# Wide up products of the later expert passes: two token blocks by two chunks with seven products

## The reference, cut to what matters

```python
def swiglu(h, w_gate, w_up, w_down):
    return (jax.nn.silu(h @ w_gate) * (h @ w_up)) @ w_down

def moe_swiglu(h, router_w, router_b, w_gate, w_up, w_down):   # D_FF_EXPERT = 1408, N_EXPERTS = 8, TOP_K = 2
    t = h.reshape(B * S, Dm)
    logits = (t @ router_w).astype(jnp.float32) + router_b.astype(jnp.float32)
    ...                                                        # combine: softmax of the two best logits
    for e in range(N_EXPERTS):
        out = out + combine[:, e:e + 1] * swiglu(t, w_gate[e], w_up[e], w_down[e])
```

## Time and profile before

| | |
|---|---|
| device time, median of three runs | 1250.8 us (1249.82 to 1252.56) |
| profiled execution: its own time | 1252.16 us |
| profiled execution: span, granted clock | 1250.6 us, 0.997 |
| busy share of TensorE, VectorE, ScalarE, GpSimd | 98%, 54%, 22%, 7% |
| bytes moved by DMA over the span | 368.62 MB, mean 295 GB/s |
| chain that ended last, by engine | TensorE 90%, VectorE 4%, DMA 3% |

### The profile page before, as it was taken

The page is one execution under the profiler, slowest core; times in us unless marked ns, Lnnn a source line. Parts: engine busy times, 40 slices in busy tenths (PEclk is TensorE's granted clock), DMA queues, the critical chain, the costliest instruction groups (busy, mean ns, idle before and its releaser), DMA issues.

```text
span 1250.6 us, 26663 instructions
## 1 busy us (share of the span) xinstructions
PE 1224.5 (98%) x10620; PEld 929.6 (74%) x10620; DVE 671.3 (54%) x1676; ACT 278.5 (22%) x739; POOL 88.4 (7%) x157
## 2 busy tenths in 40 slices
PE   6999999999999999999999999999999999999997
PEld 4758888999999867799999998777654455445444
DVE  5365563888888756556766786874541011101104
ACT  4332203311211424540000004375300000000001
POOL 0010100000000010000000000100011100110120
PEclk9999999999999999999999999999999999999999
DMA  9999884477777683146777685796599999999994
GB/s 344 413 400 415 326 304 150 167 274 274 274 257 278 242 293 126 36 166 222 276 276 281 256 320 197 292 374 177 197 384 395 416 399 398 399 422 399 399 398 175
DMA packets 74853, 368.62 MB, mean 295 GB/s; under 512 B 8739, under 2 KB 8995, under 8 KB 50082
## 3 DMA queue, kind: packets, MB, share of 16 engines
q1 hardware_dynamic: 56594, 271.22, 57.7%
q0 software_dynamic: 18192, 96.47, 20.1%
HBM read 347.60 MB, written 20.06 MB: 294 GB/s over the span
## 4 chain that ended last, share of the span: by engine, by line
PE 90%; DVE 4%; DMA 3%; ACT 1%; SPq 1%; issue 0%; DVEq 0%; POOLq 0%; ACTq 0%
PE banks L970 21%; PE banks L1298 13%; PE banks L698 13%; PE banks L957 12%; PE banks L1347 9%; PE banks L1322 5%; PE banks L723 4%; PE banks L829 2%; PE banks L787 2%; DMA side<-ada 2%; PE banks L1037 2%; PE banks L888 1%; DVE side L1744 1%; DMA ring<-stream 1%; PE banks L868 1%; PE banks L904 1%
## 5 line engine op out<-in xcount | busy, mean ns | idle before, releaser
L1744 DVE CUSTOM_DVE_ANT_0 side<-side 128x1024 f32<-128x1024 f32 x128 | 151.0, 1219 | 30.0 <-DMA side<-ada 29.9
L1298 PE MATMUL banks<-ring,arena 128*32 128x512 f32 x1536 | 166.3, 592 | 0.0
L957 PE MATMUL banks<-arena,ring 128*128 128x256 f32 x704 | 158.6, 379 | 0.0
L957 PEld LDWEIGHTS banks<-arena,ring 128*128 128x128 f32 x704 | 130.7, 190 | 16.1
L698 PE MATMUL banks<-h,ring 128*128 128x256 f32 x640 | 142.3, 381 | 0.3
L698 PEld LDWEIGHTS banks<-h,ring 128*128 128x128 f32 x640 | 119.7, 190 | 18.9 <-issue 1.8
L1298 PEld LDWEIGHTS banks<-ring,arena 128*32 128x32 f32 x1536 | 49.7, 110 | 111.5 <-issue 110.4
L2368 DVE TENSOR_TENSOR arena<-arena,banks 128x256 f32<-128x256 f32 (+1 forms) x48 | 15.2, 330 | 177.7 <-ACT arena L1681 177.7
L698 PE MATMUL banks<-arena,ring 128*128 128x256 f32 x384 | 84.3, 380 | 0.7 <-ACT arena L1480 0.5
L970 PEld LDWEIGHTS banks<-h,ring 128*128 128x128 f32 x672 | 81.4, 192 | 2.2
L970 PE MATMUL banks<-arena 128*128 128x128 f32 x672 | 81.9, 275 | 0.0
(11 more groups left out here) (334 smaller groups left out, 1547.5 us busy)
## 6 DMA issues: line engine op xcount, KB each, us to landing
ring<-stream SPq DMA_DIRECT2D x247, 512.0 KB, 5.6
ring<-experts SPq DMA_DIRECT2D x96, 1024.0 KB, 21.2
side<-ada POOLq DMA_DIRECT2D x64, 1024.0 KB, 7.4
side<-experts SPq DMA_DIRECT2D x24, 1024.0 KB, 22.9
arena<-experts SPq DMA_DIRECT2D x8, 1024.0 KB, 24.5
yrows<-side POOLq DMA_DIRECT2D x1, 6144.0 KB, 42.7
hrows<-side POOLq DMA_DIRECT2D x1, 5632.0 KB, 23.3
arena<-lasts SPq DMA_DIRECT2D x8, 512.0 KB, 24.4
```

The costliest lines, as they stand in the source:

```text
L957: last = pe.matmul(banks[:, 4 + c // 2, (c % 2) * T:(c % 2 + 1) * T], ring[:, s, c * P:(c + 1) * P], hid[:, j % 2, :], start=first and c % ...
L1298: ins = pe.matmul(banks[BLOCK * j:BLOCK * (j + 1), t, :], hg[:, t, k, :], ring[:, m, (j % 2) * 512:(j % 2 + 1) * 512], start=(k == 0), sto ...
L1744: dve.tensor_tensor_reduce(weights, weights, cond[:, 0 if layer0 else 1, :], 1.0, 0.0, ALU.mult, ALU.add, accum_out=msum[:, n:n + 1]).then ...
```

## The change

In passes 1 to 7 the wide up products of token blocks 0 and 1 are made in a form with fewer block products. Two chunks of input features (a pair, c = 0 to 3) and two token blocks form a 2x2 block matrix, and the gate and up weights of the two chunks another. Eight products of 256 columns become seven, three of them with weights as they are and four with sums of weights (`wsum`, one buffer for each of the four sums, in the memory of `h` and of `early`). VectorE makes four sums of the token blocks for the whole pass (`tksum`) and four sums of weights for each pair. It makes pair 0's sums ahead of `weighted_rows` and the others behind it. The products add up in six half banks, and nine operations of VectorE combine them (`combine_seven`). The third token block keeps its 512-column matmuls, in bank 5: first in pairs 0 to 2, last in pair 3. The narrow products move to banks 4 and 3. Wide slots are given back four at a time, near the end of a pair. GpSimd's load of the next token rows, and so what follows on its queue, waits for `s_prod`, which the first third-block matmul of pair 3 raises for the ninth time in a pass. Pass 0 keeps its old form.

```diff
+        wsum = [h[:, 0:4, :], h[:, 4:8, :], region(20, [QUADS, WIDE]), region(16, [QUADS, WIDE])]
+        tksum = var[:, :].rearrange("p (i c b) -> p i c b", i=4, b=BLOCK)
...
+        def wide_blocks(k):
+            chunk = ring[:, 2 * k:2 * k + 2, :].rearrange("p s (b n) -> p (s b) n", b=2)
+            return chunk[:, :, 0:WIDE], chunk[:, :, WIDE:2 * WIDE]
...
                 pool.wait_ge(rows_stored, 64 * (p + 1))
+                pool.wait_ge(s_prod, 9 * (p + 1))
                 pool.wait_ge(s_hg_low, p + 1)
                 rows_load(hrows[bass.ds((p + 1) * CAP, CAP), :])
...
+            def up_wide_seven(p):
+                pe.wait_ge(s_hg_low, p + 1)
+                pe.wait_ge(s_pickT_act, 1)
+                pe.wait_ge(s_tksum, 4 * p)
+                for c in range(KC // 2):
+                    (gate1, up1), (gate2, up2) = wide_blocks(2 * c), wide_blocks(2 * c + 1)
+                    start, stop = c == 0, c == KC // 2 - 1
...
+                    pe.wait_ge(slot_full[4 * c], 16 * (before[4 * c] + p + 1))
+                    if not stop:
+                        third_block(0)
+                    pe.wait_ge(slot_full[4 * c + 2], 16 * (before[4 * c + 2] + p + 1))
+                    if not stop:
+                        third_block(1)
+                    product(0, 0, hg[:, 0, 2 * c, :], gate1)
+                    product(1, 0, hg[:, 0, 2 * c + 1, :], gate2)
+                    product(2, 0, tksum[:, 3, c, :], up2)
+                    pe.wait_ge(s_wsum, 16 * p - 16 + 4 * c + 1)
+                    product(1, WIDE, tksum[:, 0, c, :], wsum[0], False)[-1].then_inc(s_prod, 1)
+                    pe.wait_ge(s_wsum, 16 * p - 16 + 4 * c + 2)
+                    product(0, WIDE, tksum[:, 1, c, :], wsum[1], False)[-1].then_inc(s_prod, 1)
+                    pe.wait_ge(s_wsum, 16 * p - 16 + 4 * c + 3)
+                    made = product(2, WIDE, tksum[:, 2, c, :], wsum[2], False)
...
+                    pe.wait_ge(s_wsum, 16 * p - 16 + 4 * c + 4)
+                    made = product(3, 0, hg[:, 1, 2 * c + 1, :], wsum[3])
+                    if stop:
+                        made[1].then_inc(s_up, 2)
+                        made[3].then_inc(s_up, 2)
+                        made = third_block(0)
+                        made[0].then_inc(s_prod, 1)
...
+                        for ins in third_block(1):
+                            ins.then_inc(s_up, 1)
...
+                def token_block_sums():
+                    dve.wait_ge(s_hg_low, p + 1)
...
+                    dve.tensor_tensor(tksum[:, 0], a21, a22, ALU.add).then_inc(s_tksum, 1)
+                    dve.tensor_tensor(tksum[:, 2], a11, a21, ALU.subtract).then_inc(s_tksum, 1)
+                    dve.wait_ge(s_tksum, 4 * p - 3)
+                    dve.tensor_tensor(tksum[:, 1], tksum[:, 0], a11, ALU.subtract).then_inc(s_tksum, 1)
+                    dve.wait_ge(s_tksum, 4 * p - 1)
+                    dve.tensor_tensor(tksum[:, 3], a12, tksum[:, 1], ALU.subtract).then_inc(s_tksum, 1)
...
+                def block_sums(c):
+                    n = 16 * p - 16 + 4 * c
+                    (gate1, up1), (gate2, up2) = wide_blocks(2 * c), wide_blocks(2 * c + 1)
+                    dve.wait_ge(slot_full[4 * c], 16 * (before[4 * c] + p + 1))
+                    if c:
+                        dve.wait_ge(s_prod, 9 * p + 2 * c - 1)
+                    dve.tensor_tensor(wsum[0], up1, gate1, ALU.subtract).then_inc(s_wsum, 1)
+                    dve.wait_ge(slot_full[4 * c + 2], 16 * (before[4 * c + 2] + p + 1))
+                    if c:
+                        dve.wait_ge(s_prod, 9 * p + 2 * c)
+                    dve.wait_ge(s_wsum, n + 1)
+                    dve.tensor_tensor(wsum[1], up2, wsum[0], ALU.subtract).then_inc(s_wsum, 1)
+                    if c:
+                        dve.wait_ge(slot_used[4 * c - 3], before[4 * c - 3] + 2 * p + 2)
+                    dve.tensor_tensor(wsum[2], up2, up1, ALU.subtract).then_inc(s_wsum, 1)
+                    if c:
+                        dve.wait_ge(slot_used[4 * c - 1], before[4 * c - 1] + 2 * p + 2)
+                    dve.wait_ge(s_wsum, n + 2)
+                    dve.tensor_tensor(wsum[3], gate2, wsum[1], ALU.subtract).then_inc(s_wsum, 1)
...
                 if first:
+                    hidden(0, 0, WIDE)
+                    hidden(1, WIDE, NARROW)
+                else:
+                    token_block_sums()
+                    block_sums(0)
                     weighted_rows(p)
-                hidden(0, 0, WIDE)
-                hidden(1, WIDE, NARROW)
+                    for c in range(1, KC // 2):
+                        block_sums(c)
+                    combine_seven()
+                    hidden_wide_seven()
+                    hidden_narrow_seven()
                 rows_turned(p)
...
             expert_pass(0, True)
+            dve.wait_ge(rows_stored, 64)
             passes = dve.value_load(ints[0:1, NTAB:NTAB + 1], min_val=EXPERTS, max_val=EXPERTS + EXTRA)
```

More of the change, by code:

```diff
@@ L1283, in combine, with up_wide @@
                                 ins.then_inc(s_lastscatter, 1)
-            def up_wide(p, first):
+            def up_wide(p):
                 pe.wait_ge(s_hg_low, p + 1)
-                if not first:
-                    pe.wait_ge(s_pickT_act, 1)
                 for k in range(KC):
-                    if first and k == 4:
+                    if k == 4:
                         pe.wait_ge(s_hg_high, 1)
@@ L1313, in up_narrow @@
                 for t in range(BLOCKS):
+                    if t == BLOCKS - 1 and not first:
+                        pe.wait_ge(s_comb, 9 * p - 8)
                     for k in range(KC):
@@ L1333, in pick_transposes, with expert_down @@
                 last.then_inc(s_picktr, 1)
-            def expert_down(p, first, last):
+            def expert_down(p, first, last, first_pass):
                 for c in range(first, last):
@@ L1351, in expert_down @@
                                 ins.then_inc(s_down, 1)
[L1352 removed]
+                            elif t == BLOCKS - 1 and m in slot_used:
                                 ins.then_inc(slot_used[m], 1)
             def expert_pass(p, first=False):
[L1356 removed]
+                if first:
+                    up_wide(p)
+                else:
+                    up_wide_seven(p)
                 up_narrow(p, first)
@@ L2381, in expert_pass @@
                     dve.wait_ge(consts_set, 6)
-                if not first:
-                    weighted_rows(p)
-                hidden(0, 0, WIDE)
-                hidden(1, WIDE, NARROW)
+                def token_block_sums():
+                    dve.wait_ge(s_hg_low, p + 1)
+                    pairs = [hg[:, t].rearrange("p (c e) b -> p c e b", e=2) for t in range(2)]
+                    a11, a12, a21, a22 = (pairs[t][:, :, e, :] for t in range(2) for e in range(2))
+                    dve.tensor_tensor(tksum[:, 0], a21, a22, ALU.add).then_inc(s_tksum, 1)
[4 more added lines that the diff above has]
+                    dve.tensor_tensor(tksum[:, 3], a12, tksum[:, 1], ALU.subtract).then_inc(s_tksum, 1)
@@ new lines, in turned, with hidden_wide_seven @@
+                def turned(t, at, w, n):
+                    dve.wait_ge(s_hid, n)
+                    dve.transpose(mhidT[:, t, at:at + w], mhid[:, t, at:at + w]).then_inc(s_hidT, 1)
+                def hidden_wide_seven():
+                    n = HIDS * p
+                    dve.wait_ge(s_msilu, n + 1)
+                    dve.tensor_tensor(mhid[:, 2, 0:WIDE], msg[:, 2, :], banks[:, 5, WIDE:2 * WIDE], ALU.mult).then_inc(s_hid, 1)
+                    for t in range(2):
+                        dve.wait_ge(s_msilu, n + t + 2)
+                        dve.wait_ge(s_comb, 9 * p)
+                        dve.tensor_tensor(mhid[:, t, 0:WIDE], msg[:, t, :], mhid[:, t, 0:WIDE], ALU.mult).then_inc(s_hid, 1)
+                        turned((2, 0)[t], 0, WIDE, n + t + 1)
+                    turned(1, 0, WIDE, n + 3)
@@ new lines, in hidden_narrow_seven @@
+                def hidden_narrow_seven():
+                    n = HIDS * p + BLOCKS
+                    for t, w in ((0, 2), (2, 1)):
+                        dve.wait_ge(s_msilu, n + t + w)
+                        dve.tensor_tensor(mhid[:, t:t + w, WIDE:QF], msg[:, t:t + w, 0:NARROW], narrow_blocks(t, w)[:, :, NARROW:2 * NARROW],
+                                          ALU.mult).then_inc(s_hid, w)
+                    for t in range(BLOCKS):
+                        turned(t, WIDE, NARROW, n + max(t, 1) + 1)
```

88 lines of the change are left out of this document (75 added, 13 removed).

## The result

The changed kernel takes 1256.29 us, the median of five runs (1255.05 to 1258.92). Its ratio to the kernel before is 1.0043, 95% interval 1.0027 to 1.0059: slower by some 5.4 us. The forecast was 1251.9 us; the time lies within the range given, but not within the forecast's own. That it lies within the range is luck: the upper end stood for slower sums of VectorE, which did not come, and the loss is another. The profiled execution took 1255.05 us, with a span of 1253.4 us and a granted clock of 0.999. It entered pass 0 2.4 us earlier than the one before, by scatter ahead of the change, so its passes lost more than the two spans show.

A forecast was written before the change was run, and what follows sets the result against it. TensorE, busy 98%, was taken to bound the kernel. Pass 1's +3.35 us less 6 x 0.37 for steady passes gave +1.1; 1253.3 for the profiled execution, 1251.9 us forecast as median, range 1248.2 to 1257.5.

The forecast's parts named there:

- the range given: Whole kernel: 1248.2 to 1257.5 us, from a time without sum stalls, with some scatter, to the sums' upper price.
- the forecast's own: Whole kernel: the favoured case's own range, 1249.5 to 1253.5 us, at a chance of 0.55.
- the upper end: VectorE's sums at their upper price, 1.28 us long and 1.20 apart; the range reaches 1257.5 us.
- Steady pass: Later passes: pair 3's last sum about 1 us late, wide part 20.2 instead of 20.60 us, gaining 0.37 a pass.
- Rival C: VectorE's sums follow each other without overlap; a pass loses 0.5 us, pass 1 4.6, time 1258.4 us; chance 0.17.
- Rival D: TensorE's clock falls in the stall of every pass, costing 1.7 us each, time about 1264 us; chance 0.08.
- Pass 1: First changed pass: late token sums and weight sums end the wide part at 964.5 instead of 961.16, losing 3.35 us.
- What costs nothing: Combining, down-part sums, moved row loads and gathers, slot returns: all hidden or in time, the gathers landing at about 1233.
- signs of being wrong: Wide part 19 us with end near 1237, sums 1.25 apart throughout, clock under 1.00 within passes, or TensorE waiting on DMA.
- The queue: Weight transfers need about 44.7 us a pass against TensorE's 42.64, falling behind 2.1 a pass; a large saving meets their end.
- rival B: Sums do not hold TensorE up, but gathered rows land about 1232.4 and mixing ends at 1237.5: 1249.0 us; chance 0.20.

The follow-up runs named there:

- one sum less: Changed kernel with VectorE's third weight sum left out in pairs 1 to 3 (output partly wrong): 1249.47 us in one run.
- gathers later: Changed kernel with GpSimd waiting for the narrow part's end after loading the rows, so the gathers fall beside the down products: 1256.42 us in one run.
- the gathers first: Changed kernel, third block first in pair 3, gathers written to ring slots and issued ahead of pass 8's unused row load: 1247.30 us, ratio 0.9977 to the kernel before.
- pass 1 written out: Changed kernel with TensorE's pass 1 written out ahead of its loop, which then starts at pass 2: 1256.61 us in one run.
- the moved wait alone: Kernel before with only POOL's new wait for the wide part's end before it loads the next rows: 1254.11 us, ratio 1.0021.
- plain loads: Changed kernel with the four indirect gathers replaced by four plain POOL loads of the same size (wrong output rows): 1253.72 us in one run.
- both edits: Changed kernel with the third block first in pair 3 and pass 1's weight and token sums made earlier: 1251.01 us, ratio 0.9995 to the kernel before.
- gathers to other memory: Changed kernel, third block first in pair 3, pass 1's sums earlier, gathers written to ring slots emptied by pair 0: 1248.03 us, ratio 0.9971 to the kernel before.
- half the weights: Changed kernel, third block first, pass 1's sums earlier, gathers to ring slots, pass 7 loading half its weight bytes (wrong output): 1241.81 us in one run.
- all together: Changed kernel, third block first, early pass 1 sums, gathers to ring slots before the unused row load, that load cut: 1244.61 us, ratio 0.9952 to the kernel before.
- third block first alone: Changed kernel with the third token block first in pair 3 too, nothing else moved: 1249.32 us, ratio 0.9987 to the kernel before.

## Why the prediction was right or wrong

**Steady pass: right.** 20.2 us of wide part were predicted, 20.16 came. The sums took 1.22 us, 1.13 to 1.20 apart where independent, 1.26 where not (1.14 and 1.25). That it fits so closely is in part luck: a group of four took 4.74 us (4.68), and VectorE began 3.51 us into the pass (3.68), and the two errors cancel. The wait in pair 3 was split, 0.3 us for the third sum and 0.5 for the fourth. Passes 2 to 7 apart from the stall gave back 0.26 + 1.79 + 0.45 = 2.50 us (2.22). Rival C is out: independent sums start before the one ahead of them has ended. The Trainium skill says in "VectorE: DVE Perf Modes", section "The DRAIN you can't avoid", that the next operation does not start until the pipeline is empty, and that one that is not held starts earlier. The trace agrees with the second part for the independent sums (1.13 to 1.20 us apart at 1.22 long); the dependent one (1.26) waits for its predecessor by a semaphore and can't tell.

**Rival D did not come in the profiled execution, but it is not out.** There the clock is 1.00 in all passes. Seven runs have the wait of 2.0 to 2.2 us for the token sums ahead of pass 1, the changed kernel among them, and in four of them the granted clock stands at 0.50 right behind it, the lower level: one sum less, gathers later, the gathers first, and pass 1 written out. With the gathers later, where TensorE and VectorE run the changed kernel's code (columns as in the earlier trace rows):

```profile
944.00:946.00 2.00, 2.00 (x12) 0.46 (x8) 2.00 (x2) 0.00 (x0) 0.00 (x0) 0.50 1.00 410
```

There the first 16 matmuls of pass 1 took 3.61 us in place of 1.92. The wide part, which waits for VectorE anyway, took 21.87 in place of 21.69 (from its first matmul to the first narrow one).

**Pass 1: right in the wide part, short behind it.** Predicted were 3.35 us; the wide part lost 3.15. The down part lost 0.87 more in a stall on the loop's first turn. Pass 0, priced at nothing, lost 0.79 in small gaps of its narrow and down parts. That need not be the change: with the moved wait alone, where pass 0 is that of the kernel before, it lost 1.48.

**The step that failed is "What costs nothing".** "Behind that POOL wait also stand the last row loads and gathers, which move from 1207.8 to about 1217." That came as described (1216.80, the gathers from 1219.57). The bytes landed in time too: VectorE mixed from 1231.21 on, ahead of TensorE's end at 1242.07. I asked only that, and not what TensorE runs beside them. Beside the old wide products of 512 columns they cost nothing; beside the narrow ones TensorE lost 2.96 us (2.51 + 0.45). The moved wait alone reproduces it in the kernel before, plain loads take it away, and a later issue moves it into the down part. None of the signs of being wrong that I had named would have caught it. It is the largest piece of the miss: predicted +1.1, measured +5.26; the difference of 4.1 is 2.96 for the gathers, 0.87 and 0.79 for the gaps in passes 1 and 0, less 0.48 for what the wide part of pass 1 and the steady passes did better.

**The queue: right, and more important than I made it.** From the earlier trace rows I had 44.7 us of transfers a pass. In the changed kernel a ring load of pass 1 lands after 12.2 us and one of pass 6 after 25.2 (DMA issues, medians), no later than before:

```profile
ring<-experts SPq DMA_DIRECT2D x12, 1024.0 KB, 12.2
...
ring<-experts SPq DMA_DIRECT2D x12, 1024.0 KB, 25.2
```

That is (25.2 - 12.2) / 5 = 2.6 us a pass behind a pass of 42.2. At 41.0, with pass 1 shortened too, the lead is gone in pass 6 or 7, as the waits for weights in four runs show (both edits, gathers to other memory, half the weights, all together); with half of pass 7's bytes those of pass 7 are gone. With the third block first alone there is no such wait. So rival B's end was real, though the changed kernel never reached it: with the third block first the sums hold nothing up, the chain runs over the gathered rows, and the time is 1249.32 us, where B had 1249.0.

## What to carry to other kernels

When an edit moves a wait on one queue, look at what every transfer behind it will then run beside, not only at when it lands; an indirect gather that was free beside one kind of product cost 3 us beside another. Where a transfer queue falls behind its consumer by a steady amount a pass, its total and not the consumer sets what a faster consumer can win, once the lead is used up. Put work that needs no late operand ahead of work that does: the third block's place in one pair of four decided 1.2 us a pass.

## What the hardware did that I had not expected

Indirect gathers held up matmuls in groups of five, 0.73 us a group, in the narrow part (192 columns), the down part and the wide part of one run (256 columns). It was not so with plain loads of the same size in one run, nor beside the old products of 512 columns, nor in the wide part of the last kernel, where the queue was full, nor in that of the run with half the weights. The gathers and a full queue were there in each stall, but they do not suffice. Late code is no cause, since no instruction packets move then. What TensorE waits for is shown by no row: this stays open.

While gathers move, the DMA engines are as busy as ever and carry less: in the kernel with both edits 1.02 and 426 GB/s at 1208 to 1209 us, 1.02 and 270 at 1215 to 1216. That is not of their kind: with plain loads it is 1.01 and 244 at 1222 to 1223, without a stall of TensorE.

Four idle microseconds ahead of the combining took TensorE's clock to its lower level, and the combining took 2.7 us longer (5.58 against 2.87). Being early was worse there than being late. After the 2 us of idle ahead of pass 1 the clock fell in four of seven runs.
